# The gates' narrow slot one place earlier in a first projection, their rows' chain beside it, and two items scaled ahead of convolutions

## The reference

```python
aq, ak, av, ao, ai, af, bq, bkc, bvc, bks, bvs, bkw, bvw, bg = _split(h @ w_in, EVEN_SIZES)
ya = _mlstm(aq, ak, av, ao, ai + a_i_b, af + a_f_b, a_conv, a_norm)
yb = _nsa(bq, bkc, bvc, bks, bvs, bkw, bvw, bg + b_g_b, b_cmp_pos, b_cmp_w1, b_cmp_w2)
return jnp.concatenate([ya, yb], -1) @ w_out
```

## Time and profile before

| | before |
|---|---|
| median of 3 runs | 3453.35 us (3449.25 to 3454.97) |
| the profiled execution | 3446.24 us |
| its span | 3444.9 us |
| PE busy | 95% |
| DVE, ACT, POOL busy | 59%, 43%, 30% |
| DMA queues' share | 27.5% |

### The profile page before, as it was taken

The page is one execution under the profiler, slowest core; times in us unless marked ns, Lnnn a source line. Parts: engine busy times, 40 slices in busy tenths (PEclk is TensorE's granted clock), DMA queues, the critical chain, the costliest instruction groups (busy, mean ns, idle before and its releaser), DMA issues.

```text
span 3444.9 us, 47895 instructions
## 1 busy us (share of the span) xinstructions
PE 3276.9 (95%) x20089; PEld 2898.1 (84%) x20092; DVE 2015.5 (59%) x3021; ACT 1471.9 (43%) x2256; POOL 1029.6 (30%) x460
## 2 busy tenths in 40 slices
PE   8898999999879999989999999999999999999999
PEld 6786789987667899978999878999999998789998
DVE  4557555463683644557566635855685567357556
ACT  4454344443342544445444332533453443235433
POOL 3120124332421233321333332223323333323233
PEclk9999999999999999999999999999999999999999
DMA  3310323321112223221332312233323323232332
GB/s 128 101 50 1 110 74 115 106 104 56 56 43 74 80 98 111 98 92 50 123 129 74 118 66 92 92 99 104 113 72 115 112 86 110 74 98 82 94 111 75
DMA packets 239815, 308.98 MB, mean 90 GB/s; under 512 B 8336, under 2 KB 168096, under 8 KB 239088
## 3 DMA queue, kind: packets, MB, share of 16 engines
q1 hardware_dynamic: 236016, 291.41, 25.7%
q0 software_dynamic: 3584, 14.52, 1.1%
HBM read 303.80 MB, written 2.10 MB: 89 GB/s over the span
## 4 chain that ended last, share of the span: by engine, by line
PE 76%; DVE 18%; ACT 4%; issue 2%; DMA 0%; POOL 0%; DVEq 0%; ACTq 0%
PE bank L591 24%; PE bank L593 23%; PE bank L592 23%; DVE wlo L2005 2%; ACT whi L1276 1%; PE bank L611 1%; DVE wraw L2027 1%; DVE wkk_o L2811 1%; DVE raw_w L2027 1%; ACT P_e L1587 1%; DVE gb L2808 1%; PE bank L931 1%; DVE uv_x L2941 1%; DVE h L2047 1%; DVE h L2060 1%
## 5 line engine op out<-in xcount | busy, mean ns | idle before, releaser
L3065 POOL TENSOR_TENSOR wlo<-wraw,whi 128x1024 fp32r<-128x1024 f32 (+3 forms) x246 | 632.1, 2573 | 1474.0 <-ACT whi L1276 1473.7
L591 PE MATMUL bank<-xh,whi 128*128 128x256 f32 (+1 forms) x2456 | 721.6, 294 | 27.0 <-DVE xl L2280 12.3
L1276 ACT ACTIVATE whi<-wraw 128x1024 fp32r<-128x1024 f32 (+3 forms) x426 | 440.2, 1038 | 712.8 <-PE bank L593 567.2
L593 PE MATMUL bank<-xh,wlo 128*128 128x256 f32 (+1 forms) x2456 | 716.7, 292 | 0.0
L592 PE MATMUL bank<-xl,whi 128*128 128x256 f32 (+1 forms) x2456 | 713.0, 290 | 0.0
L3065 POOL TENSOR_TENSOR wlo<-raw_w,whi 128x1024 fp32r<-128x1024 f32 (+1 forms) x148 | 358.0, 2422 | 766.3 <-ACT whi L1276 766.3
L591 PEld LDWEIGHTS bank<-xh,whi 128*128 128x128 f32 x2456 | 465.4, 189 | 45.5 <-issue 18.0
L591 PE MATMUL bank<-whi,uh_w 128*128 128x512 f32 x1216 | 475.1, 391 | 0.0
L592 PEld LDWEIGHTS bank<-xl,whi 128*128 128x128 f32 x2456 | 465.6, 190 | 10.5
L593 PE MATMUL bank<-whi,ul_w 128*128 128x512 f32 x1216 | 474.0, 390 | 0.0
L592 PE MATMUL bank<-wlo,uh_w 128*128 128x512 f32 x1216 | 474.0, 390 | 0.0
(11 more groups left out here) (401 smaller groups left out, 5254.8 us busy)
## 6 DMA issues: line engine op xcount, KB each, us to landing
wraw<-in_w_in SPq DMA_DIRECT2D x26, 1024.0 KB, 5.1
wraw<-in_ffn_w_down SPq DMA_DIRECT2D x20, 1024.0 KB, 5.0
raw_w<-in_ffn_w_down SPq DMA_DIRECT2D x20, 1024.0 KB, 5.0
raw_w<-in_mlp_w SPq DMA_DIRECT2D x19, 1024.0 KB, 5.4
wraw<-in_mlp_w SPq DMA_DIRECT2D x17, 1024.0 KB, 5.3
wraw<-in_ffn_w_gate SPq DMA_DIRECT2D x32, 512.0 KB, 4.3
raw_w<-in_ffn_w_gate SPq DMA_DIRECT2D x32, 512.0 KB, 4.7
raw_w<-in_ffn_w_up SPq DMA_DIRECT2D x32, 512.0 KB, 4.7
```

Of the source, the lines that this page charges most:

```text
L591: M.matmul(o, lh, rh, start=start, stop=False, skip_group_check=more)
L593: return M.matmul(o, ll, rh, start=False, stop=stop, skip_group_check=more)
L1276: A.activation(hi, raw, ACT.Copy).then_inc(*k.w_hi.inc(("hi", j)))
L3065: G.tensor_tensor(lo[:, 0:n], raw[:, 0:n], hi[:, 0:n].bitcast(F), ALU.subtract).then_inc(*k.w_lo.inc(("lo", j)))
```

## The change

In the plan of weights, `e_g` moves from behind the fourth `e_in` slot to between the third and the fourth, and every engine's program follows. ACT evicts the gates' rows and does Abs and Exp before feature 6's eviction, Ln behind it, and then feature 7's and those of `e_vs`. DVE does the bias additions between `windows(0)` and `windows(1)`, and the whole rows' chain ahead of the `kl` subtractions. PE's and ACT's waits for the constants come a slot later. In the item loop DVE does `scaled` of items 0 and 1 before that iteration's unit instead of after it.

```diff
--- before.py
+++ after.py
@@ -328,8 +328,9 @@
                 plan.slot(tag, v[:, k:kn, c:min(c + 512, c1)], fine)
 
     v = kview("e_w_in")
-    add_fm("e_in", v, 0, 1024)
+    add_fm("e_in", v, 0, 768)
     plan.slot("e_g", v[:, :, 3328:3424])
+    add_fm("e_in", v, 768, 1024)
     add_fm("e_vs", v, 1024, 1280)
     for j in range(2):
         plan.slot("cmp", I["e_b_cmp_w1"][j].rearrange("p (k c) -> p k c", c=128))
@@ -772,8 +773,7 @@
 
     def even():
         e = k.even
-        fm("e_in", [[("e_in", 2 * n), ("e_in", 2 * n + 1)] for n in range(4)], x, need=lambda kk: ("x", kk))
-        pe.wait_ge(at("con"))
+        fm("e_in", [[("e_in", 2 * n), ("e_in", 2 * n + 1)] for n in range(3)], x, need=lambda kk: ("x", kk))
 
         j = slots.get("e_g")
         wh, wl = weights(j)
@@ -782,6 +782,8 @@
             i = mm3(bank[0:96, :], wh[:, kk, :], wl[:, kk, :], xh[:, kk, :], xl[:, kk, :], kk == 0, kk == 7)
         i.then_inc(*made.inc(("made", ("e_g",)), ("used", j)))
         slots.done()
+        fm("e_in", [[("e_in", 6), ("e_in", 7)]], x)
+        pe.wait_ge(at("con"))
 
         run(tm_units("e_vs", ("e_vs",), 256, x))
         pe.wait_ge(at("g_rows"))
@@ -1473,9 +1475,7 @@
                 else:
                     A.activation(e.kh[own, i - 6, g, :], src, ACT.Copy).then_inc(*done.inc(("ks hi", i - 6, g)))
                     A.activation(e.kh[other, i - 6, g, :], src, ACT.Copy).then_inc(*done.inc(("ks hi twice", i - 6, g)))
-        fm("e_in", [[("e_in", 2 * n), ("e_in", 2 * n + 1)] for n in range(4)], e_in)
-        act.wait_ge(at("con"))
-        act.wait_ge(at("eps"))
+        fm("e_in", [[("e_in", 2 * n), ("e_in", 2 * n + 1)] for n in range(3)], e_in)
 
         slots.get("e_g")
         slots.done()
@@ -1484,15 +1484,23 @@
         A.activation(e.g_rows, bank[0:24, :], ACT.Copy).then_inc(*done.inc(("g_rows",)))
         A.activation(e.r_i, bank[32:36, :], ACT.Copy)
         A.activation(e.r_f, bank[64:68, :], ACT.Copy).then_inc(*done.inc(("r_f",), ("free", ("e_g",))))
-        def e_vs(key, tt):
-            copy_out(key, e.vsw[:, tt, :, :, 0, :], ring.of(key)[:, 0:256].rearrange("p (a g d) -> p a g d", a=2, g=2), ("vsw one", tt))
-        run(tm_units("e_vs", ("e_vs",), e_vs))
+        slots.prepare()
         act.wait_ge(at("r_f bias"))
         A.activation(e.r_ls, e.r_f, ACT.Abs).then_inc(*done.inc())
         act.wait_ge(done.now())
         A.activation(e.r_ls, e.r_ls, ACT.Exp, scale=-1.0).then_inc(*done.inc(("r_ls exp",)))
-        act.wait_ge(at("r_ls one"))
-        A.activation(e.r_ls, e.r_ls, ACT.Ln).then_inc(*done.inc(("r_ls ln",)))
+
+        def e_in_ln(key):
+            e_in(key)
+            if key[1] == 6:
+                act.wait_ge(at("r_ls one"))
+                A.activation(e.r_ls, e.r_ls, ACT.Ln).then_inc(*done.inc(("r_ls ln",)))
+        fm("e_in", [[("e_in", 6), ("e_in", 7)]], e_in_ln)
+        act.wait_ge(at("con"))
+        act.wait_ge(at("eps"))
+        def e_vs(key, tt):
+            copy_out(key, e.vsw[:, tt, :, :, 0, :], ring.of(key)[:, 0:256].rearrange("p (a g d) -> p a g d", a=2, g=2), ("vsw one", tt))
+        run(tm_units("e_vs", ("e_vs",), e_vs))
         act.wait_ge(at("r_bM"))
         A.activation(e.r_em, e.r_b, ACT.Exp, scale=-1.0).then_inc(*done.inc(("r_em",)))
         act.wait_ge(at("gts bias"))
@@ -2327,13 +2335,12 @@
 
         fm("e_in", [[("e_in", 4), ("e_in", 5)]], e_in)
         windows(0)
-        fm("e_in", [[("e_in", 6), ("e_in", 7)]], e_in)
-        windows(1)
         slots.skip("e_g", 1)
         slots.prepare()
         dve.wait_ge(at("r_f"))
         V.tensor_scalar_add(e.r_i, e.r_i, par[0:4, P_IB:P_IB + 1])
         V.tensor_scalar_add(e.r_f, e.r_f, par[0:4, P_FB:P_FB + 1]).then_inc(*done.inc(("r_f bias",)))
+        windows(1)
         dve.wait_ge(at("r_ls exp"))
         V.tensor_scalar_add(e.r_ls, e.r_ls, 1.0).then_inc(*done.inc(("r_ls one",)))
         V.memset(e.r_one, 1.0).then_inc(*done.inc())
@@ -2352,6 +2359,7 @@
         dve.wait_ge(done.now())
         V.scalar_tensor_tensor(e.nmr[32:36, :], e.r_M, -1.0, e.nmr[0:4, :].bitcast(F), ALU.mult, ALU.subtract).then_inc(*done.inc(("nmr",)))
         V.tensor_tensor(e.r_b, e.r_b, e.r_M, ALU.add).then_inc(*done.inc(("r_bM",)))
+        fm("e_in", [[("e_in", 6), ("e_in", 7)]], e_in)
 
         run(tm_units("e_vs", ("e_vs",), lambda key, tt: None))
         dve.wait_ge(at("made", ("gts",)))
@@ -2528,8 +2536,10 @@
         for n in range(N + 2):
             if n < N:
                 first(n)
+            if n < 2:
+                scaled(n)
             next(units, None)
-            if n < N:
+            if 2 <= n < N:
                 scaled(n)
             if n >= 12 and n % 3 == 0:
                 next(units, None)
@@ -3111,8 +3121,9 @@
         slots.ahead = 1
         G.memset(e.vx[:, :, :, 128:130], 1.0).then_inc(*done.inc(("vx ones",)))
         G.dma_start(e.w2, I["w2"]).then_inc(*k.landed["w2"].inc(("w2",)))
-        slots.skip("e_in", 4)
+        slots.skip("e_in", 3)
         slots.skip("e_g", 1)
+        slots.skip("e_in", 1)
         slots.get("e_vs")
         for tt in range(NT):
             pool.wait_ge(at("vsw one", tt))
```

## The result

The changed kernel takes 3439.6 us in the median of 6 runs (3437.73 to 3445.68), the kernel before 3450.6 us in 6 runs beside them. The ratio is 0.9971 with a 95% interval of 0.9961 to 0.9982: some 10 us less (6 to 13). A later measurement, 12 runs of the changed kernel and 17 of the kernel before, gave 0.9973 (0.9964 to 0.9981). The predicted difference was 10.6 us. As will be seen, its two halves were both wrong, by about 2.5 us each, in opposite directions.

A forecast was written before the change was run, and what follows sets the result against it. TensorE is busy for 95% of the span, so only its waits and the slow clock after them can be won: -4.6 us up to e_qk's second feature and -6.0 at the first items, -10.6 to 3442.7 us; range 3436.5 to 3448.

The forecast's parts named there:

- The wait before the last `e_in` slot: PE waits 1.7 us for POOL's low half there, where 3.62 us stood before e_vs: -1.9 us.
- Its clock: After the 1.7 us wait before the last e_in slot PE's full clock is kept: another -1.65 us.
- rival 2: The 1.7 us wait loses the clock and DVE comes 1.5 to 2 us later: -8.5 to -7 us; chance 13%.
- DVE's queue comes late next: Before e_qk's first slot, DVE's half of the low weights is done at 85.0; PE waits 2.4 us.
- so I count a drop, +1.6: The new wait before e_qk's first slot loses the clock, costing 1.6 us.
- the first part's 4.6: Gain up to e_qk's second feature from moving the slot and the rows' chain: -4.6 us.
- The stop of a chain operation: POOL's work on e_qk's first slot stops a DVE rows' chain operation until 78.0; without it, 82.7 and no PE wait.
- The GELU wait: PE's 3.50 us wait for ACT's GELU of the hidden rows goes: -3.5 us, and its slow clock -1.6.
- The 2.07 us wait: PE's wait before e_qk's second slot, for a split ACT reaches after the kc eviction, stays with its slow clock.
- The first two items: Item loop: scaled(1) at about 147.8 removes PE's 3.48 us wait, leaving about 0.3 us for PT(0).
- -5.9, say -6.0 us: Item 3's transposes begin at 159.8 instead of 165.7, clock included; gain bounded by 4 below and 7 above.
- if items 2 and 3 wait: Sign in PE's timeline that the prediction is wrong: waits at items 2 and 3 of the item loop.

The follow-up runs named there:

- the tests above: Changed kernel with DVE doing half of the last e_in slot's low weights (wait before e_qk 3.54 us), or POOL all of e_qk's first slot's (no wait there).
- the shared slot: Changed kernel with DVE doing half of the last e_in slot's low weights ahead of windows(0); e_g's end to hidden(1) 44.9 us against 42.5.
- each part alone: On the kernel before: slot and rows' chain moved without the scaling, 3442.4 us (0.9979); only scaled of items 0 and 1 moved, 3448.6 us (0.9994).
- the one with the old chain: Changed kernel with the rows' chain back where it was on DVE and ACT; 3446.6 us, ratio 0.9990 to the kernel before.

## Why the prediction was right, and where it was not

**The total** was right, -10.6 us against some -10. **The wait before the last `e_in` slot**: 1.7 us predicted, 1.86 measured, ended by POOL; right. **Its clock**: kept, as taken, but not as safely as that sounds. The prediction's rows had 1.50 us kept and 1.84 us lost, and 1.86 us lies past both. Its reason, dense matmuls in place of small tiles, fits the traces: a wait of 1.83 to 1.87 us lost the clock here in two of nine, and at one place among small tiles beyond 200 us in all fourteen. In the changed kernel's second trace it was lost after the same 1.86 us, and there rival 2's absorption can be seen: 3.4 us at half clock, then no wait before `e_qk`'s first slot at all, and `hidden(1)` 48.2 us behind the `kvT` eviction instead of 48.0. PE came later to a half that DVE hadn't finished anyway, so the slow clock cost 0.2 us. The windows:

```profile
56.20:59.60 3.40, 3.40 (x10) 0.52 0.74 289
83.00:99.50 16.50, 16.50 (x95) 1.00 0.37 128
```

**DVE's queue comes late next**: right as a mechanism (the tests above move it both ways). The term was mis-sized: DVE's half was done 1.2 us after PE came, not 2.4. DVE's queue took 34.7 us from its first window, not 35.6 (the first windows with their stop 8.60 for 9.3, the additions with theirs 5.2 for 5.6), and PE came 0.3 us later than reckoned, counted from the same window. And **"so I count a drop, +1.6"** failed: a wait of 1.31 to 1.37 us stood there in six traces, and all six kept the clock. These two are 2.7 us, and with them the first part's 4.6 is the 7.0 us measured (7.5 between the marks, less 0.5 of the start). **The stop of a chain operation** was open; it came, at 72.97. The Trainium skill, SBUF — State Buffer, § Who interferes with whom, has a VectorE instruction with two SBUF inputs and a GpSimd one that reads SBUF exclude each other for a whole instruction; this trace agrees, with 2.82 us for an operation of 0.68, beside POOL's 2.40. **The GELU wait** went, as predicted. **The 2.07 us wait** stayed, as predicted.

**The first two items**: "-5.9, say -6.0 us" failed. 3.55 us were measured, under the lower bound of 4. Scaled P was in time, and the 0.4 us for PT(0) was right (0.3 predicted). What the step left out is the bank: the ring comes to feature 7's bank for item 3's scores, and convolution 7 frees it 1.0 us too late, since it stands behind a low half that waits for ACT's split, which waits for PE. With the clock behind it that is 2.7 us. The prediction checked the ring for the `kl` banks and not here. By two of its own signs it is wrong in this half: "if items 2 and 3 wait", and the clock, which was to be full at items 1 to 3. That the total came out at 10 us all the same is luck.

## What to carry to other kernels

When a short piece of work moves away from a long preparation, the next short cover is what to look at, and after it the in-order queue of the engine that now holds the moved chain: a wait of PE that such a queue ends doesn't shrink when PE comes earlier, as the shared slot showed. With a ring of banks, ask at each removed wait which bank is taken next and which instruction frees it. Two errors of 2.5 us cancelled here, and the total would never have told; only each part alone and marks in the trace did.

## What was unexpected in the hardware

The same wait in the same place does not always cost the clock. The 1.85 us wait at 54 us lost it in two of the nine traces that have it (this kernel's second trace and the one with the old chain), the 1.0 us wait at item 3 in seven of nine, and the 2.07 us wait in eight of ten. With POOL doing all of the first `e_qk` slot the last two were both kept:

```profile
101.00:104.40 3.40, 3.40 (x15) 1.00 1.07 352
144.30:149.60 5.30, 5.30 (x45) 1.00 0.67 198
```

So between 1.0 and 2.1 us the length of a wait alone doesn't decide. What does decide was not tried; the traces show only what went with it. The two that lost the clock at 54 us are those in which PE's first matmuls came to their fast pace earliest (15.6 and 15.7 us; the other seven at 17.0 to 18.6). The two that kept it behind the 2.07 us wait are those in which PE hadn't waited 0.3 us or more for over 40 us before; in the eight others a wait of 1.3 to 5.0 us had ended 12 to 18 us before.

Nor does a slow stretch of 3.4 us always cost the same. Half of it, 1.7 us, is the most; the next wait takes its part. Between marks around each, a lost clock cost 0.2 us at 54 (the wait before `e_qk`'s first slot went), 0.4 to 0.5 us behind the 2.07 us wait (the traces that kept it waited 0.93 and 1.02 us for `hidden(1)`'s GELU instead), and 1.5 us at item 3, where no wait followed.
